# A transformer trunk on one core: the last two experts' rows by one-hot products, the other rows reloaded in two waves, the last norm on VectorE

## The chip, the core and the metric

The kernel runs on one core of a Trainium2 chip. Five engines work side by side: TensorE (products into eight PSUM banks of 128x512), VectorE, ScalarE, GpSimd (POOL) and SyncE (SP), which in this kernel only issues transfers. Each engine runs its own list of instructions in order and waits for the others through semaphores. The metric is the device time of one execution in microseconds, the median of several runs.

## The reference

One layer over 512 tokens of width 1024. After a mixer (pooling, chunked attention, a state space) comes a first LayerNorm, which gives h. The part that matters here is the second half:

```python
def moe(h, combine, w_gate, w_up, w_down):
    out = jnp.zeros_like(h)
    for e in range(N_EXPERTS):
        a = jax.nn.silu(h @ w_gate[e]) * (h @ w_up[e])
        out = out + combine[..., e:e + 1].astype(h.dtype) * (a @ w_down[e])
    return out
...
        combine = route(h, w_router, router_bias)
        ffn = moe(h, combine, w_exp_gate[i], w_exp_up[i], w_exp_down[i])
        ple = jax.nn.sigmoid(h @ w_ple_gate[i]) * (p[i] @ w_ple_proj[i])
        x = layer_norm(DN_ALPHA * h + ffn + ple, ln2_g[i], ln2_b[i])
```

There are 16 experts with an inner width of 256. route gives every token two experts and two weights that sum to one; combine is zero elsewhere. A token's ffn is therefore the weighted sum of two rows.

## The kernel before

The 512 tokens are four row tiles (t = 0 to 3) of 128 tokens. `xh` (region_f) holds alpha * h + ple of all four by the time the experts begin.

Each expert has room for 128 tokens (CAP); overflow goes to up to 7 extra rounds under `If(n_over > 0)`, which the inputs here do not enter. VectorE works out the slot of each (token, k) pair, k = 0 or 1 being the first and second expert of the token. GpSimd writes the pair's number 2 * token + k into `inv_d` at its slot with eight indirect transfers (line 530) and reads the list back as `inv_t`; `tok_t` is inv_t shifted right by one. For each expert GpSimd gathers the token rows of h from `h_d` (line 538) and, when the expert is done, scatters its 128 result rows to `ye_d` (expert_scratch) at the pair's number (line 543). Rows of ye_d are unweighted, and each is written by exactly one expert.

TensorE goes through the experts in a software pipeline: gate and up products of expert e (lines 1194 to 1207), the transposes of the tokens of e + 1 (1178), the down products of e - 1 (1222), the transposes of the activation of e (1212). fp32 operands are split into an upper and a lower part of a cheaper type (fp32r); ScalarE writes the upper parts (lines 797, 804, 819, 823), VectorE the lower ones (1664 to 1679). `step` is VectorE's share of one expert. The semaphore pe_dn counts finished down products. The results stand in banks 1 and 2 (B_DN), those of expert 15 in banks 4 and 5 (B_TOK). ScalarE copies them to `y_e` (line 831), expert e - 1 after its work for expert e. For expert 15 VectorE copies one half (1704) and ScalarE the other (844).

When the last scatter has landed, GpSimd sets moe_done, and SyncE reloads ye_d in eight transfers of 512 KB, one for each t and k (line 409). Then, per row tile: VectorE adds the two weighted rows to xh (`combine`, line 1728) and takes the mean; ScalarE squares and sums (`deviation`, 860) and takes the root (863). For tiles 0 and 1 ScalarE normalises (`x_hat`, 867) and VectorE multiplies by the gain and adds the bias (`affine`, 1746 and 1747); for tiles 2 and 3 VectorE does both with two instructions (1754, 1757) around a reciprocal. SyncE stores each tile (412). `ln_st`, `ln_mv`, `ln_rs` hold sum, mean and square sum, and root and its reciprocal.

## Time and profile before

| what | us |
|---|---|
| median of 3 runs | 471.43 (471.35 to 471.88) |
| the profiled execution | 470.61, its span 468.9 |
| TensorE busy | 426.5 (91%) |
| VectorE busy | 321.5 (69%) |
| ScalarE busy | 218.4 (47%) |
| GpSimd busy | 116.0 (25%) |
| share of the chain that ended last | TensorE 86%, VectorE 5%, ScalarE 3%, DMA 3% |

The span goes from the first to the last recorded instruction of the one profiled execution; the rest of its time lies around it. The chain is followed back from the last instruction, at each step to what released it. "Landing" is the time from a transfer's issue to its semaphore. Numbers in the sections below are of this one execution unless they are called a median.

### The profile page before, as it was taken

What the parts mean: (1) busy time and instruction counts of PE and PEld (TensorE: products, weight loads), DVE (VectorE), ACT (ScalarE), POOL (GpSimd) and SP (SyncE); (2) the same over time, 40 slices, a digit from 0 to 9 for tenths busy, and PEclk for the clock granted to TensorE, in tenths of its full rate; (3) what the DMA queues carried; (4) which work ended last, traced back from release to release, by engine and by line L of the source; (5) the groups of instructions that cost most, each with busy time, mean ns of one, the idle gap of its engine ahead of it and who ended that gap; (6) DMA issues with size and microseconds to landing.
All of it is one profiled execution on the core that took longest, in us unless ns stands there. A gap on an engine that the chain in (4) does not pass through costs nothing.

```text
span 468.9 us, 5180 instructions
## 1 busy us (share of the span) xinstructions
PE 426.5 (91%) x1837; PEld 280.1 (60%) x1837; DVE 321.5 (69%) x491; ACT 218.4 (47%) x361; POOL 116.0 (25%) x145
## 2 busy tenths in 40 slices
PE   6999999999999999999999999999999999999000
PEld 2444564496675544446687676777777777777000
DVE  3799959876343876667483257787767777777287
ACT  3111361053976800115110157788677787786151
POOL 7880051560085100000006500222332222212000
PEclk9999999999999999999999999999999999999655
DMA  8992032327965701112620249999999999610563
GB/s 275 381 365 91 0 52 71 75 89 217 414 266 198 295 0 45 45 46 67 254 83 0 54 166 426 407 422 419 408 374 364 390 370 389 249 72 16 184 258 144
DMA packets 36792, 98.95 MB, mean 211 GB/s; under 512 B 16049, under 2 KB 22081, under 8 KB 30113
## 3 DMA queue, kind: packets, MB, share of 16 engines
q1 hardware_dynamic: 27472, 88.01, 49.4%
q0 software_dynamic: 5600, 8.94, 5.7%
...
q14 instruction: 11, 0.08, 0.0%
...
## 4 chain that ended last, share of the span: by engine, by line
PE 86%; DVE 5%; ACT 3%; DMA 3%; issue 1%; SPq 0%; POOLq 0%; DVEq 0%
PE bank L885 12%; PE bank L1049 11%; PE bank L1222 10%; PE bank L1194 5%; PE bank L892 5%; PE bank L1199 4%; PE bank L1203 4%; PE bank L1207 4%; PE bank L1121 3%; PE bank L1123 3%; PE bank L1122 3%; PE bank L1135 3%; PE bank L1178 3%; PE bank L901 2%; DVE region_f L1728 2%; PE bank L910 2%
## 5 line engine op out<-in xcount | busy, mean ns | idle before, releaser
L1049 PE MATMUL bank<-region_b,region_e 128*128 128x512 f32 x128 | 58.3, 601 | 0.6 <-DVE region_f L1521 0.6
L885 PE MATMUL bank<-region_e,region_a 128*128 128x512 f32 x128 | 55.9, 595 | 0.0
L885 PEld LDWEIGHTS bank<-region_e,region_a 128*128 128x128 f32 x128 | 24.1, 190 | 29.4 <-issue 29.1
L1049 PEld LDWEIGHTS bank<-region_b,region_e 128*128 128x128 f32 x128 | 23.2, 191 | 25.0 <-issue 23.6
L1199 PE MATMUL bank<-gate_up_upper,tokens_upper 128*128 128x512 f32 x96 | 36.3, 459 | 0.0
L530 POOL DMA_INDIRECT slot_scratch<-io_t,slot_i x8 | 8.4, 1055 | 93.4 <-issue 93.4
L543 POOL DMA_INDIRECT expert_scratch<-region_g,inv_t x8 | 11.5, 1436 | 78.2 <-ACT region_g L831 78.2
L1672 DVE TENSOR_TENSOR gate_up_lower<-region_a,gate_up_upper 128x1024 fp32r<-128x1024 f32 x24 | 28.0, 1221 | 2.7 <-ACT gate_up_upper L804 2.7
L1203 PE MATMUL bank<-gate_up_upper,tokens_lower 128*128 128x512 f32 x96 | 29.8, 392 | 0.0
L892 PE MATMUL bank<-region_e,region_a 128*128 128x512 f32 x48 | 23.4, 651 | 4.7 <-DMA region_a<-in_w_in 4.7
L1121 PE MATMUL bank<-ple_gate_upper,hidden_upper 128*128 128x512 f32 x64 | 26.6, 415 | 0.0
L1521 DVE SCALAR_TENSOR_TENSOR region_f<-bank,rms_r,region_f 128x512 f32<-128x512 f32 x24 | 18.0, 750 | 11.6 <-PE bank L1049 11.0
L1123 PE MATMUL bank<-ple_gate_upper,hidden_lower 128*128 128x512 f32 x64 | 25.0, 391 | 0.0
L1122 PE MATMUL bank<-ple_gate_lower,hidden_upper 128*128 128x512 f32 x64 | 25.0, 390 | 0.0
L804 ACT ACTIVATE gate_up_upper<-region_a 128x1024 fp32r<-128x1024 f32 x24 | 23.7, 1058 | 2.6 <-DMA region_a<-in_w_exp_down 2.6
L1207 PE MATMUL bank<-gate_up_lower,tokens_upper 128*128 128x512 f32 x96 | 24.5, 391 | 0.0
L1199 PEld LDWEIGHTS bank<-gate_up_upper,tokens_upper 128*128 128x128 f32 x96 | 18.1, 189 | 10.4 <-issue 6.0
L543 POOL DMA_INDIRECT expert_scratch<-region_b,inv_t x8 | 10.2, 1276 | 49.4 <-ACT region_b L831 40.1
L772 ACT ACTIVATE ln_rs<-ln_mv,eps_t 128x1 f32<-128x1 f32 x4 | 1.2, 296 | 45.4 <-DVE ln_mv L1527 45.4
L768 ACT ACTIVATE region_h<-bank 128x512 f32<-128x512 f32 x8 | 4.8, 597 | 37.4 <-PE bank L1123 37.4
L901 PE MATMUL bank<-region_a,region_e 128*128 128x384 f32 x64 | 21.2, 488 | 0.0
L1203 PEld LDWEIGHTS bank<-gate_up_upper,tokens_lower 128*128 128x128 f32 x96 | 18.0, 188 | 4.0
...
## 6 DMA issues: line engine op xcount, KB each, us to landing
...
```

What stands on the lines that cost most here:

```text
L885: last = mm(bank[bank_i][:], w[:, k, m * P:(m + 1) * P], xT[:, k, :], start=(k == 0), stop=(k == KD - 1))
L892: last = mm(bank[m][:], w_ssm[:, k, m * P:(m + 1) * P], xT[:, k, :], start=(k == 0), stop=(k == KD - 1))
L901: last = mm(bank[bank_i][:, 0:ATT_W], xT[:, k, t * P:(t + 1) * P], w_v[:, k, :], start=(k == 0), stop=(k == KD - 1))
L1049: last = mm(bank[WO_AT[half][group]][:], hdT[:, k, t * P:(t + 1) * P], w_o[:, k, half * 512:half * 512 + 512], start=(i == 0), stop=(i == ...
L1121: mm(bank[PG_AT[k % 2]][:], h_hi[t][:, x], pg_hi[:, w], start=(c == 0), stop=False)
L1122: mm(bank[PG_AT[k % 2]][:], h_hi[t][:, x], pg_lo[:, w], start=False, stop=False)
L1123: last = mm(bank[PG_AT[k % 2]][:], h_lo[t][:, x], pg_hi[:, w], start=False, stop=(c == KD - 1))
L1199: mm(out_, x_hi[r][:, k * P:(k + 1) * P], w_hi[:, k], start=False, stop=False)
L1203: mm(out_, x_lo[:, k * P:(k + 1) * P], w_hi[:, k], start=False, stop=False)
L1207: last = mm(out_, x_hi[r][:, k * P:(k + 1) * P], w_lo[:, KD - KS + k], start=False, stop=(k == KS - 1))
L1222: last = mm(bank[banks[half]][:], x[r][:, k * P:(k + 1) * P], w[:, k * D + half * 512:k * D + half * 512 + 512], start=(i == 0), stop=(i = ...
L1672: tt(w_lo[:, :, at:at + 2 * DE], w[:, :, at:at + 2 * DE], w_hi[:, :, 2 * c * DE:2 * (c + 1) * DE], ALU.subtract).then_inc(S["gu_lo_set"], 1)
```

## The change

- The pair written to the slot list is now (number, weight), so that the list read back, `inv_w`, holds for each slot its weight. ScalarE's copies out of the banks (now lines 871 to 875) scale by it, and ye_d holds weighted rows.
- Experts 14 and 15 (LATE = 2) are not scattered. ScalarE writes the upper part of their weighted rows to `yl_hi`, VectorE the lower part to `yl_lo`. VectorE builds for each of the two a one-hot matrix `onehot` of 128 slots by 512 tokens from a row of token numbers, `t_iota`. TensorE multiplies them, for each row tile, into the banks of OH_BANKS.
- Since the rows of these two experts are no longer written, ye_d is filled with zeros first: a tile of zeros goes to `zero_d`, and eight transfers from there to ye_d stand in SyncE's list ahead of the stores of h.
- The reload begins when the scatters up to expert 13 have landed. First wave, on SyncE: both k of tiles 0 and 1, into `y_two` (k = 1) and `y_one` (k = 0). Second wave, when tile 0 is there: k = 1 of tiles 2 and 3 on SyncE, k = 0 of tiles 2 and 3 by two transfers of GpSimd that add to xh.
- y_two goes into the banks by products with the identity, ahead of the one-hot products of the same tile. y_one is added to xh by VectorE.
- combine adds a tile's two banks to xh with an accumulator. The norm of all four tiles is made with the two instructions that tiles 2 and 3 had; x_hat and affine are gone.

The diff, cut to its core:

```diff
 OVER = 7
+LATE = 2
...
+OH_BANKS = ((3, 6), (7, 0), (1, 2), (4, 5))
...
+        y_two = RB[:, 4096:8192].rearrange("p (t d) -> p t d", t=NT)
+        y_one = RA[:, 2048:4096].rearrange("p (t d) -> p t d", t=2)
+        t_iota = RH[:, 7168:7168 + T]
+        onehot = [over(f"onehot{i}", T, C0 + 4 * (8192 + i * T)) for i in range(LATE)]
+        yl_hi = [over(f"late_upper{i}", D, B0 + 4 * (2 * i * D)) for i in range(LATE)]
+        yl_lo = [over(f"late_lower{i}", D, B0 + 4 * ((2 * i + 1) * D)) for i in range(LATE)]
...
+            sp.dma_start(zero_d, RH[:, 3072:3072 + D]).then_inc(S["ye_zero"], 16)
+            sp.wait_ge(S["ye_zero"], 16)
             sp.wait_ge(S["kern_done"], 2)
...
+            for c in range(2 * NT):
+                sp.dma_start(ye_d[c * P:(c + 1) * P, :], zero_d).then_inc(S["ye_zero"], 16)
...
+            yv = ye_d.rearrange("(t p k) d -> t k p d", p=P, k=2)
+            sp.wait_ge(S["pe_dn"], NE - LATE)
+            for b in range(4):
+                sp.wait_ge(S[f"ye_out{b}"], 16 * ((NE - LATE - 1 - b) // 4 + 1))
+            for t in range(2):
+                sp.dma_start(y_two[:, t, :], yv[t, 1]).then_inc(S[f"y_in{t}"], 16)
+                sp.dma_start(y_one[:, t, :], yv[t, 0]).then_inc(S[f"y_in{t}"], 16)
+            sp.wait_ge(S["y_in0"], 32)
+            for t in range(2, NT):
+                sp.dma_start(y_two[:, t, :], yv[t, 1]).then_inc(S["y2_in"], 16)
...
-            sp.wait_ge(S["moe_done"], 1)
-            yv = ye_d.rearrange("(t p k) d -> t k p d", p=P, k=2)
-            for t in range(NT):
-                for k in range(2):
-                    sp.dma_start(RA[:, (2 * t + k) * D:(2 * t + k + 1) * D], yv[t, k]).then_inc(S[f"yk{k}_in{t}"], 16)
...
+            link(g.iota(t_iota, pattern=[[1, T]], base=0, channel_multiplier=0, allow_small_or_imprecise_dtypes=True))
...
-                if e == NE - 1:
-                    gp.wait_ge(S["ye_last"], 1)
-                    gp.wait_ge(S["ye_evac"], 2 * e + 1)
-                else:
+                if e < NE - LATE:
                     gp.wait_ge(S["ye_evac"], 2 * e + 2)
-                scatter(inv_t[:, e:e + 1], y_e[e % 4], f"ye_out{e % 4}")
+                    scatter(inv_i[:, e, 0:1], y_e[e % 4], f"ye_out{e % 4}")
             n_over = gp.value_load(over_i[0:1, 0:1], min_val=0, max_val=OVER)
             for b in range(4):
-                gp.wait_ge(S[f"ye_out{b}"], 16 * NE // 4)
+                gp.wait_ge(S[f"ye_out{b}"], 16 * ((NE - LATE - 1 - b) // 4 + 1))
+            gp.wait_ge(S["ple_done"], 2 * NT)
+            yv = ye_d.rearrange("(t p k) d -> t k p d", p=P, k=2)
+            gp.wait_ge(S["y_in0"], 32)
+            for t in range(2, NT):
+                gp.dma_start(xh[:, t, :], yv[t, 0], accum_op=ALU.add).then_inc(S[f"y_in{t}"], 16)
...
-                    a.activation(y_e[b][:, half * 512:half * 512 + 512], bank[B_DN[half]][:], ACT.Copy).then_inc(S["ye_evac"], 1)
+                    a.activation(y_e[b][:, half * 512:half * 512 + 512], bank[B_DN[half]][:], ACT.Copy,
+                                 scale=inv_w[:, e, 1:2]).then_inc(S["ye_evac"], 1)
+
+            def late_upper(i, half, banks):
+                a.activation(yl_hi[i][:, half * 512:half * 512 + 512], bank[banks[half]][:], ACT.Copy,
+                             scale=inv_w[:, NE - LATE + i, 1:2]).then_inc(S["yh_set"], 1)
...
-                if e >= 1:
+                if 1 <= e < NE - 1:
                     y_copy(e - 1, (0, 1))
-            ac.wait_ge(S["pe_dn"], NE + 1)
-            ac.wait_ge(S["ye_out3"], 16 * (NE // 4 - 1))
-            a.activation(y_e[3][:, 512:1024], bank[B_TOK[1]][:], ACT.Copy).then_inc(S["ye_evac"], 1)
+            ac.wait_ge(S["pe_dn"], NE - 1)
+            for half in range(2):
+                late_upper(0, half, B_DN)
+            for half in range(2):
+                ac.wait_ge(S["pe_dn"], NE + half)
+                late_upper(1, half, B_TOK)
...
-            def x_hat(t):
-                ac.wait_ge(S["rs2_ready"], t + 1)
-                a.activation(xh[:, t, :], xh[:, t, :], ACT.Identity, bias=ln_mv[:, t, 0:1], scale=ln_rs[:, t, 1:2]).then_inc(S["xhat_done"], 1)
-
             a.preload_act_table(ACT.Sqrt)
-            deviation(0)
-            deviation(1)
-            x_hat(0)
-            deviation(2)
-            x_hat(1)
-            deviation(3)
+            for t in range(NT):
+                deviation(t)
...
+            def to_tokens(t, half, i, start, stop):
+                for n_, y in enumerate((yl_hi[i], yl_lo[i])):
+                    last = mm(bank[OH_BANKS[t][half]][:], onehot[i][:, t * P:(t + 1) * P], y[:, half * 512:half * 512 + 512],
+                              start=(start and n_ == 0), stop=(stop and n_ == 1))
+                return last
+
+            def both_halves(t, i, stop):
+                for half in range(2):
+                    if i == 1 and t == 0:
+                        pe.wait_ge(S["yh_set"], 3 + half)
+                        pe.wait_ge(S["yl_set"], 5 + half)
+                    last = to_tokens(t, half, i, False, stop)
+                return last
+
+            for t in range(NT):
+                if t < 2:
+                    pe.wait_ge(S[f"y_in{t}"], 32)
+                else:
+                    pe.wait_ge(S["y2_in"], 32)
+                if t == NT - 1:
+                    pe.wait_ge(S["yh_set"], 4)
+                    pe.wait_ge(S["yl_set"], 6)
+                for half in range(2):
+                    mm(bank[OH_BANKS[t][half]][:], ident[:], y_two[:, t, half * 512:half * 512 + 512], start=True, stop=False)
+                if t == 0:
+                    pe.wait_ge(S["yh_set"], 2)
+                    pe.wait_ge(S["yl_set"], 4)
+                both_halves(t, 0, False)
+                both_halves(t, 1, True).then_inc(S["pe_dn"], 1)
...
+                link(tt(pair_w[:, :, k, 1], wgt[:, k, :], wsum, ALU.mult))
+            link(v.tensor_copy(pair_i[:, :, 0], io_t[:]))
...
+            def late_lower(i, half, banks):
+                dv.wait_ge(S["yh_set"], 2 * i + half + 1)
+                cols = slice(half * 512, half * 512 + 512)
+                stt(yl_lo[i][:, cols], bank[banks[half]][:], inv_w[:, NE - LATE + i, 1:2], yl_hi[i][:, cols],
+                    ALU.mult, ALU.subtract).then_inc(S["yl_set"], 1)
+
             for e in range(NE - 4, NE):
                 step(e, e % 4, last=(e == NE - 1))
-            dv.wait_ge(S["pe_dn"], NE)
-            dv.wait_ge(S["ye_out3"], 16 * (NE // 4 - 1))
-            v.tensor_copy(y_e[3][:, 0:512], bank[B_TOK[0]][:]).then_inc(S["ye_last"], 1)
+                if e < NE - 2:
+                    i = e - (NE - 4)
+                    ts(onehot[i][:], t_iota, tok_f[:, i:i + 1], None, ALU.is_equal).then_inc(S["yl_set"], 1)
+            for i, banks in enumerate((B_DN, B_TOK)):
+                for half in range(2):
+                    late_lower(i, half, banks)
+            for t in range(2):
+                dv.wait_ge(S[f"y_in{t}"], 32)
+                if t == 0:
+                    dv.wait_ge(S["ple_done"], 2 * NT)
+                tt(xh[:, t, :], xh[:, t, :], y_one[:, t, :], ALU.add).then_inc(S["one_added"], 1)
+            dv.wait_ge(S["one_added"], 2)
...
             def combine(t):
 
-                for k in range(2):
-                    dv.wait_ge(S[f"yk{k}_in{t}"], 16)
-                    yk = RA[:, (2 * t + k) * D:(2 * t + k + 1) * D]
-                    link(stt(xh[:, t, :], yk, wgt[:, k, t:t + 1], xh[:, t, :], ALU.mult, ALU.add,
-                             accum_out=ln_st[:, t, 0:1] if k == 1 else None))
-                ts(ln_mv[:, t, 0:1], ln_st[:, t, 0:1], -1.0 / D, None, ALU.mult).then_inc(S["z2_ready"], 1)
-
-            def scale_rows(t):
-
+                if t >= 2:
+                    dv.wait_ge(S[f"y_in{t}"], 16)
+                dv.wait_ge(S["pe_dn"], NE + 1 + t + 1)
+                for half in range(2):
+                    cols = slice(half * 512, half * 512 + 512)
+                    link(stt(xh[:, t, cols], bank[OH_BANKS[t][half]][:], 1.0, xh[:, t, cols], ALU.mult, ALU.add,
+                             accum_out=ln_st[:, t, half:half + 1]))
+                ts(ln_mv[:, t, 0:1], ln_st[:, t, 0:1], ln_st[:, t, 1:2], -1.0 / D, ALU.add, ALU.mult).then_inc(S["z2_ready"], 1)
+
+            def centred(t):
+                return RE[:, t * D:(t + 1) * D]
+
+            def centre(t):
+                dv.wait_ge(S["z2_ready"], t + 1)
+                link(stt(centred(t), xh[:, t, :], ln_mv[:, t, 0:1], lng2, ALU.add, ALU.mult))
+
+            def scale(t):
                 dv.wait_ge(S["ln_sqrt"], NT + t + 1)
                 link(v.reciprocal(ln_rs[:, t, 1:2], ln_rs[:, t, 0:1]))
-                tt(ln_mv[:, t, 0:1], ln_mv[:, t, 0:1], ln_rs[:, t, 1:2], ALU.mult).then_inc(S["rs2_ready"], 1)
+                stt(xh[:, t, :], centred(t), ln_rs[:, t, 1:2], lnb2, ALU.mult, ALU.add).then_inc(S["o_dve"], 1)
 
             combine(0)
+            centre(0)
+            scale(0)
             combine(1)
-            scale_rows(0)
+            centre(1)
+            scale(1)
             combine(2)
-            scale_rows(1)
-
-            def affine(t):
-                dv.wait_ge(S["xhat_done"], t + 1)
-                link(tt(xh[:, t, :], xh[:, t, :], lng2, ALU.mult))
-                tt(xh[:, t, :], xh[:, t, :], lnb2, ALU.add).then_inc(S["o_dve"], 1)
-
-            affine(0)
+            centre(2)
             combine(3)
-            affine(1)
-            for t in range(2, NT):
-                xg = RE[:, (t - 2) * D:(t - 1) * D]
-                link(stt(xg, xh[:, t, :], ln_mv[:, t, 0:1], lng2, ALU.add, ALU.mult))
-                dv.wait_ge(S["ln_sqrt"], NT + t + 1)
-                link(v.reciprocal(ln_rs[:, t, 1:2], ln_rs[:, t, 0:1]))
-                stt(xh[:, t, :], xg, ln_rs[:, t, 1:2], lnb2, ALU.mult, ALU.add).then_inc(S["o_dve"], 1)
+            scale(2)
+            centre(3)
+            scale(3)
```

SyncE's end of list. Before, behind the overflow block, which itself waits for all down products:

```order
L395 REGISTER_ALU
L395 COMPARE_AND_BRANCH
L394 UNCONDITIONAL_BRANCH
L409 DMA region_a<-expert_scratch 128x1024 [waits moe_done]
L409 DMA region_a<-expert_scratch 128x1024 x7
L412 DMA out<-region_f 128x1024 [waits o_dve] x4
```

Now, from the last weight load on, ahead of that block:

```order
L408 DMA region_c<-in_w_exp_down 128x2048 [waits pe_dn]
L415 DMA region_b<-expert_scratch 128x1024 [waits ye_out2,ye_out1,ye_out3,ye_out0,pe_dn]
L416 DMA region_a<-expert_scratch 128x1024
L415 DMA region_b<-expert_scratch 128x1024
L416 DMA region_a<-expert_scratch 128x1024
L419 DMA region_b<-expert_scratch 128x1024 [waits y_in0]
L419 DMA region_b<-expert_scratch 128x1024
```

The reloads moved ahead of the overflow block and of the wait for the last down product; they wait for the scatters (ye_out0 to ye_out3, one per buffer) instead.

VectorE before, from the first reloaded tile on:

```order
L1728 SCALAR_TENSOR_TENSOR region_f<-region_a,wgt,region_f 128x1024 [waits yk0_in0,ln2_in]
L1728 SCALAR_TENSOR_TENSOR region_f,ln_st<-region_a,wgt,region_f 128x1024 [waits yk1_in0,dve_step]
L1730 TENSOR_SCALAR ln_mv<-ln_st 128x1 [waits dve_step]
L1728 SCALAR_TENSOR_TENSOR region_f<-region_a,wgt,region_f 128x1024 [waits yk0_in1]
L1728 SCALAR_TENSOR_TENSOR region_f,ln_st<-region_a,wgt,region_f 128x1024 [waits yk1_in1,dve_step]
L1730 TENSOR_SCALAR ln_mv<-ln_st 128x1 [waits dve_step]
L1735 RECIPROCAL ln_rs<-ln_rs 128x1 [waits ln_sqrt]
L1736 TENSOR_TENSOR ln_mv<-ln_mv,ln_rs 128x1 [waits dve_step]
L1728 SCALAR_TENSOR_TENSOR region_f<-region_a,wgt,region_f 128x1024 [waits yk0_in2]
L1728 SCALAR_TENSOR_TENSOR region_f,ln_st<-region_a,wgt,region_f 128x1024 [waits yk1_in2,dve_step]
```

VectorE now, after its last lower part of the expert phase (region_a is y_one), and from the first combine on (late_upper_83 and late_lower_85 are expert 14's parts, the next numbers expert 15's):

```order
L1777 SCALAR_TENSOR_TENSOR late_lower_85<-bank,region_h,late_upper_83 128x512 [waits yh_set] x2
L1777 SCALAR_TENSOR_TENSOR late_lower_86<-bank,region_h,late_upper_84 128x512 [waits yh_set] x2
L1792 TENSOR_TENSOR region_f<-region_f,region_a 128x1024 [waits ple_done,y_in0]
L1792 TENSOR_TENSOR region_f<-region_f,region_a 128x1024 [waits y_in1]
L1794 TENSOR_LOAD over_i [waits one_added]
```

```order
L1821 SCALAR_TENSOR_TENSOR region_f,ln_st<-bank,region_f 128x512 [waits pe_dn,ln2_in]
L1821 SCALAR_TENSOR_TENSOR region_f,ln_st<-bank,region_f 128x512 [waits dve_step]
L1823 TENSOR_SCALAR ln_mv<-ln_st 128x1 [waits dve_step]
L1830 SCALAR_TENSOR_TENSOR region_e<-region_f,ln_mv,region_h 128x1024 [waits z2_ready]
L1834 RECIPROCAL ln_rs<-ln_rs 128x1 [waits ln_sqrt,dve_step]
L1835 SCALAR_TENSOR_TENSOR region_f<-region_e,ln_rs,region_h 128x1024 [waits dve_step]
L1821 SCALAR_TENSOR_TENSOR region_f,ln_st<-bank,region_f 128x512 [waits pe_dn]
```

Two reads of reloaded rows per tile became one read of two banks, and the load of the overflow count (TENSOR_LOAD over_i) now stands behind the two sums that wait for the reload.

TensorE before ended with the down products of expert 15:

```order
L1222 MATMUL bank<-down_upper_last,act_upper_78 128x512 x2
L1222 MATMUL bank<-down_lower_72,act_upper_78 128x512 x2
L1222 MATMUL bank<-down_upper_last,act_lower_80 128x512 x2
L1275 TENSOR_LOAD over_i
L1275 ISA x2
L1278 COMPARE_AND_BRANCH [waits ye_last,ye_evac]
```

Now its list goes on behind the overflow block (region_b is y_two; tile 0 and the start of tile 1):

```order
L1316 UNCONDITIONAL_BRANCH
L1355 MATMUL bank<-region_b,ident 128x512 [waits y_in0]
L1355 MATMUL bank<-region_b,ident 128x512
L1334 MATMUL bank<-late_upper_83,onehot_81 128x512 [waits yl_set,yh_set]
L1334 MATMUL bank<-late_lower_85,onehot_81 128x512
L1334 MATMUL bank<-late_upper_83,onehot_81 128x512
L1334 MATMUL bank<-late_lower_85,onehot_81 128x512
L1334 MATMUL bank<-late_upper_84,onehot_82 128x512 [waits yl_set,yh_set]
L1334 MATMUL bank<-late_lower_86,onehot_82 128x512
L1334 MATMUL bank<-late_upper_84,onehot_82 128x512 [waits yl_set,yh_set]
L1334 MATMUL bank<-late_lower_86,onehot_82 128x512
L1355 MATMUL bank<-region_b,ident 128x512 [waits y_in1]
```

Four such groups of ten stand there, one per row tile.

## Rows read from the trace of the kernel before

**Rows 1.** Windows: busy us of each engine, granted clock, DMA share, GB/s.

```profile
434.08:439.08 5.00, 0.00 (x1) 0.00 (x0) 0.00 (x0) 1.88 (x2) 0.97 (x1) 0.73 0.29 115
...
442.43:465.82 23.39, 0.00 (x0) 0.00 (x0) 21.21 (x30) 8.41 (x14) 0.00 (x0) 0.50 0.55 212
465.82:468.90 3.08, 0.00 (x0) 0.00 (x0) 0.00 (x1) 0.00 (x0) 0.00 (x0) 0.50 0.42 170
```

**Rows 2.** Chain of waits: start us, us, what; from the last scatter on.

```profile
435.55 3.19 DMA expert_scratch<-region_b,inv_t
...
439.08 0.33 SPq L409
...
439.93 6.85 DMA region_a<-expert_scratch
...
446.81 1.28 DVE region_f L1728
...
448.17 1.30 DVE region_f L1728 x2
```

**Rows 3.** Timeline: start us, us, engine, line; the last experts.

```profile
418.36 0.41 DVE L1658 TENSOR_TENSOR region_c<-region_c,bank 128x256 f32<-128x256 f32 x1
...
426.50 1.43 POOL L543 DMA_INDIRECT expert_scratch<-region_g,inv_t  x1 [7.19 <-ACT region_g L831]
...
434.12 0.60 ACT L844 ACTIVATE region_b<-bank 128x512 f32<-128x512 f32 x1 [2.12 <-PE bank L1222]
435.54 1.28 ACT L869 ACT_TABLE_LOAD   x1 [0.83 <-issue]
```

**Rows 4.** Tile expert_scratch, 426 to 427: landing of expert 13's scatter alone.

```profile
DMA to landing us min/median/max: 3.6/3.6/3.6
```

**Rows 5.** Timeline: one tile's sums and norm, and a last product.

```profile
442.43 2.61 DVE L1728 SCALAR_TENSOR_TENSOR region_f<-region_a,wgt,region_f 128x1024 f32<-128x1024 f32 x2 [8.98 <-DMA region_a<-expert_scratch]
...
445.08 0.15 DVE L1730 TENSOR_SCALAR ln_mv<-ln_st 128x1 f32<-128x1 f32 x1
...
446.54 0.30 ACT L863 ACTIVATE ln_rs<-ln_mv,eps_t 128x1 f32<-128x1 f32 x1
...
461.82 1.28 DVE L1757 SCALAR_TENSOR_TENSOR region_f<-region_e,ln_rs,region_h 128x1024 f32<-128x1024 f32 x1
```

**Rows 6.** VectorE's groups by form: count, busy us, mean ns, idle before.

```profile
L1521 DVE SCALAR_TENSOR_TENSOR region_f<-bank,rms_r,region_f 128x512 f32<-128x512 f32 x24 | 18.0, 750 | 11.6 <-PE bank L1049 11.0
...
L1747 DVE TENSOR_TENSOR region_f<-region_f,region_h 128x1024 f32<-128x1024 f32 x2 | 2.4, 1224 | 0.1
```

**Rows 7.** Chain of waits: products of both kinds on TensorE.

```profile
266.18 0.23 PE bank L1122
...
266.64 3.43 PE bank L1135 x8
```

**Rows 8.** Line 409: landing of the eight reloads.

```profile
DMA to landing us min/median/max: 3.3/8.1/10.6
```

**Rows 9.** Windows of TensorE: its busy us, granted clock, DMA share, GB/s.

```profile
436.40:436.60 0.20, 0.00 (x0) 0.54 0.00 0
```

**Rows 10.** Waits of SyncE: us in total, times, longest.

```profile
SPq L310 <- ACT region_c L658: 39.8, 1, 39.8
```

**Rows 11.** Windows, all engines: the stretch after expert 0's first loads.

```profile
165.00:170.00 5.00, 4.40 (x14) 1.97 (x13) 3.51 (x6) 0.57 (x3) 0.00 (x0) 1.00 0.00 0
```

**Rows 12.** Timeline: SyncE's stores of h, VectorE, the first gather, its reader.

```profile
176.88 42.95 SPq L369 DMA_DIRECT2D h_scratch<-region_f  x4
...
221.45 0.69 DVE L1543 SCALAR_TENSOR_TENSOR region_f<-region_f,region_h 128x512 f32<-128x512 f32 x1
...
263.89 1.45 POOL L538 DMA_INDIRECT region_e<-h_scratch,tok_t  x1 [4.56 <-DVE tok_t L1649]
...
269.91 1.05 PE L1178 MATMUL bank<-ident,region_e 128*128 128x128 f32 x8
```

**Rows 13.** Tile region_e, GpSimd, 263 to 265: landing of the first gather.

```profile
DMA to landing us min/median/max: 4.6/4.6/4.6
```

58 lines of the change are left out of this document (40 added, 18 removed).

## Prediction

> **What bounds the kernel now.** I read the page's list of engines first. TensorE is busy for nine tenths of the span, so the body of the kernel is TensorE's and only the end can be anyone else's. The windows of the last 40 us show where that stops: TensorE ends at 434.08, five us follow in which VectorE does nothing, VectorE is then busy for 21.2 of 23.4 us, and the last 3.1 us are a store alone [rows 1]. The chain of waits names the steps: the last expert's rows are sent to memory (435.55, 3.19 us to landing), SyncE then issues the reloads from 439.08, the third of them takes 6.85 us, and from 446.81 the chain is VectorE to 465.82 [rows 2]. Before 434 the chain is the experts' matmuls without a gap worth naming. So a gain can come from three things only: when the reload starts, how long VectorE works after it, and the last store.
>
> **The change: the reload.** Before, the reload waits for the last scatter. Now it waits for expert 13's. That scatter is issued at 426.50 and lands 3.6 us later [rows 3, 4], so the first wave is issued at 430.15 instead of 439.08. Its four transfers of 512 KB have the first four of the eight as their measure: the third landed 7.73 us after the first issue (446.81 - 439.08), the fourth no later than 448.11, where its reader begins (448.17 less the two short steps between), or 9.03 us [rows 2]. Token tile 1 is complete at 430.15 + 7.73 to 9.03 = 437.9 to 439.2; I take 438.4, nearer the low end, because only four transfers share the engines instead of eight. Tile 0 is complete by about 430.15 + 4.6 = 434.8 (VectorE's two reads of it in before began 442.43 and about 443.7) [rows 5]. Nothing else uses the DMA engines then: the weight loads are over.
>
> The late evacuations: ScalarE's last one ends at 434.72, as before [rows 3]. VectorE's lower part of it is a 128x512 product from a bank, 0.75 us by the same kind of instruction [rows 6], so it ends at 435.5. It replaces a copy of about the same length. Then VectorE adds tile 0 (1.22 us, a 128x1024 sum [rows 6]), to 436.8, and waits for tile 1: 438.4 + 1.25 = 439.65. Then it loads the overflow count and branches. No row of VectorE shows that price; ScalarE's same pair stands as 0.83 us of idle before its table load [rows 3]. The bounds are 0 and 0.83; I take 0.83, since nothing here reads ahead of the wait. The first product sum therefore starts at 440.5 and not at 442.43.
>
> **VectorE's work.** A row tile now costs two 128x512 sums from banks with accumulator (0.75 and 0.08 to read it, and gaps of 0.04), and a 0.15 us scalar: 1.95 us. Before it was 2.80 (442.43 to 445.23) [rows 5]. Centring is one 1.28 us instruction; ScalarE's square, its accumulator and its root are over at 446.84, and the sum ended at 445.23: 1.61 us and a gap of 0.03, 1.64 [rows 5]. So for tiles 0 and 1, where VectorE waits for the root before it goes on, a tile is 1.95 + 1.64 + 1.50 (reciprocal, as short as the scalar's 0.15, last product 1.28, and gaps [rows 5]) = 5.09, twice 10.2. For tiles 2 and 3 the order is sum 2, centre 2, sum 3, scale 2, centre 3, scale 3, and the root of tile 3 is hidden by 2.8 us of work: 1.95 + 1.34 + 1.95 + 1.50 + 1.31 + 1.47 = 9.5. Together 19.7 us against the 23.4 of before. The end is 440.5 + 19.7 = 460.2, and the store adds 3.08 as before [rows 1]: **a span of 463.3 against 468.9, 5.6 us less**.
>
> **What must hide for that.** TensorE now makes 8 fp32 identity products and 32 one-hot products. By the chain a fp32 product of this size takes 3.43 / 8 = 0.43 us and one of the split kind 0.23 [rows 7]. A tile is 2 x 0.43 + 8 x 0.23 = 2.7 us. Tile 0's products wait for the last lower part (435.5) and end near 437.5, three us before VectorE wants them at 440.5. Tile 1 starts at 438.4 and ends 441.1, wanted at 445.6. The second wave (tiles 2 and 3) is issued at 434.8 by SyncE and GpSimd. Before, the last of the eight reloads was issued at 442.5 and landed at most 10.6 us later [rows 8], so all 4 MB were there 14.0 us after the first issue; the same from 430.15 is 444.2. VectorE wants tile 2 at 440.5 + 10.2 = 450.7 and tile 3 at 454.0. So the two adding transfers have 7 us of room. No row shows such a transfer. From below its price is that of a plain GpSimd transfer alone, 3.2 to 3.6 us [rows 2, 4]; from above I allow three times that after a start at 436, 447, still in time.
>
> The clock is the second cover. TensorE's granted clock fell from 1.0 to 0.5, from the level of 2.4 GHz to that of 1.2, at about 436.5, when the engine had done nothing for 2.4 us [rows 9]. Here it pauses 0.7 us at 434.1 and about 1 us at 437.5, so I expect the high level through tile 1. If it falls, a tile takes some 5.4 us (twice the rows above, an estimate): tile 1 ends 443.8, tile 2 449.2, tile 3 454.6, which VectorE wants at 454.0. That costs 0.6 us, not more.
>
> The Trainium skill, "TensorE: Matmul & The Clock Gate" (the part on HAM oscillation), says that work in bursts shorter than the wait between them runs at the low level every time. By that rule all four tiles would be slow and the end 0.6 us later, 463.9 instead of 463.3; the trace shows one such fall, after one long pause, and bears the rule out only so far.
>
> **Edits earlier in the kernel, taken at nothing.** The fill of the scratch tensor: one 512 KB store of zeros early on SyncE, ahead of copies for which SyncE had waited 39.8 us anyway [rows 10], and eight 512 KB copies from memory to memory before the stores of h. DMA was idle from 165 to 170 [rows 11]; the stores of h were issued from 176.88, and VectorE's first use of what they guard is at 221.45 [rows 12]. 4 MB read and written from 165 at the latest may last 50 us before anyone waits. The pair of slot and weight: one more VectorE copy (some 0.2 us) and a wider payload of 8 bytes in the same number of pieces. The first gather was issued at 263.89 and landed 4.6 us later, 268.5; TensorE reaches its tokens at 269.91 [rows 12, 13]. 1.4 us of cover, of which 0.2 is used. The weight as ScalarE's scale costs nothing that I can see. The two one-hot builds (at most the 0.75 us of the 128x512 form in [rows 6]) stand on VectorE after steps 12 and 13. VectorE had no pause before 418.36 [rows 3], so the next product is up to 0.75 us later; TensorE wants it only after the twelve down products that stand ahead, 12 x 0.23 = 2.8 us [rows 7].
>
> **The rivals.**
> First, **the products for tiles 2 and 3 become the bound**: low clock and a late second wave together. For it: TensorE's work comes in four bursts, and the second wave is shared by two queues. If the plain half of it lands at 446 and not by 444.2, tile 2 ends 451.4 and tile 3 456.8, against 454.0: +2.8. With clock alone +0.6. Time 466.4 to 468.6.
> Second, **the other side: adding transfers that crawl**. The place is VectorE's sum of tile 3, behind GpSimd's second transfer. The gain is gone when that one lands at 454.0 + 5.6 = 459.6, 23 us after its issue, against 3.2 for a plain one: seven times slower. At 27 us the kernel takes 475. Nothing in the profile speaks for seven times, but nothing shows the operation either.
> Third, **the head pays**: copies from memory to memory so slow that the h stores land after 221, or the slot list comes back over 1.4 us later. Each further us is one us on TensorE. With 1 to 3 us of this: 466.8 to 468.8; a loss needs 5.6.
> Fourth, **the early reload does not happen early**, since one of SyncE's waits before it is later than I read: then only VectorE's 23.4 - 19.7 = 3.7 us are gained, 467.7.
>
> **How the numbers follow.** The profiled execution took 470.61 with its span of 468.9; the median of the three runs is 471.43, and I take 5.6 us from that: 471.43 - 5.6 = **465.8**. Chances: forecast 0.64 (464.3 to 467.0), first rival 0.16, second 0.08 (of which 0.05 ends slower than before), third 0.07 (0.02 slower), fourth 0.05. The low end: no price for the count (-0.8) and tile 1 at 437.9 (-0.5), together 464.5, and 0.2 for the spread of the runs. The high end takes in the first and fourth rival: 468.6. A measurement of this kernel can tell about 0.2% from no change, 0.94 us, so same means 470.5 to 472.4. Faster 0.88, same 0.05, slower 0.07.
>
> **What would show it.** The first reload issued within half a us of 430.2; VectorE's first sum from a bank at 440 to 441 and its last instruction near 460.2; pauses of VectorE between the sums of tiles 2 and 3 under 1 us, ended by ScalarE and not by TensorE or a DMA; a granted clock of 1.0 to about 441; TensorE's last down product still at 434.1. Wrong would be a last down product later than 434.5 (then the head or the one-hot builds cost), a wait of VectorE for region_f from the scratch tensor (adding transfers), or one for a bank (TensorE).

## The result, and the profile after

The changed kernel takes 464.56 us (median of 4 runs, 463.55 to 464.59), the kernel before 471.39 beside it (4 runs, 471.04 to 471.88). The ratio of the runs is 0.9849 with a 95% interval of 0.9833 to 0.9864: 7.1 us faster (6.4 to 7.9; the medians alone differ by 6.8), where 5.6 was forecast. The profiled execution took 464.56 with a span of 462.8, against 470.61 and 468.9: 6.1 us of span.

First the windows of the changed kernel's last 28 us (columns as in [rows 1]): from the last down product to VectorE's first sum from a bank, from there to VectorE's end, and the last store.

```profile
434.90:441.38 6.48, 5.17 (x18) 3.13 (x17) 3.27 (x5) 1.97 (x2) 1.89 (x2) 1.00 0.92 304
441.38:459.76 18.38, 9.65 (x33) 5.76 (x31) 17.02 (x32) 6.14 (x12) 0.00 (x0) 0.95 0.55 159
459.76:462.80 3.04, 0.00 (x0) 0.00 (x0) 0.00 (x0) 0.00 (x0) 0.00 (x0) 0.50 0.43 172
```

Set beside [rows 1], the 23.39 us from VectorE's first sum to its end have become 18.38, and its busy time 17.02 instead of 21.21. The gap ahead is shorter too (6.48 against 8.35, from 434.08 to 442.43), though this execution's last down product ended 0.8 us later than before's. The last store is as it was. Counted from the last down product, 5.0 us are gained in the stretch and 1.9 in the gap ahead of it.

The chain of waits of the changed kernel, from the issue of the fourth reload on (start, us, what; to be read beside [rows 2]):

```profile
432.25 6.59 DMA region_a<-expert_scratch
438.87 1.24 DVE region_f L1792
...
440.13 0.56 DVEq L1794
...
440.73 0.22 DVEq L1794
...
441.38 0.71 DVE region_f L1821 x2
442.11 0.71 DVE region_f L1821 x2
442.84 0.23 DVE ln_mv L1823
443.09 1.25 ACT region_a L908 x2
...
458.48 1.28 DVE region_f L1835
```

The first bank sum is only 1.05 us earlier than the first sum of before, though the reload starts 8.15 us earlier. Before, VectorE began 3.35 us after the first issue, with tile 0, and waited for tile 1 in between; now it waits for tile 1 (7.9 us after the first issue), adds it (1.24) and loads the count (1.28), 10.45 us in all. What is bought with the longer way to the first sum is a shorter stretch after it.

By the timeline the first reload was issued at 430.93 ([rows 2] had 439.08). In the chain, the second half of tile 1's rows lands at 438.84, and between the add and the first bank sum stand 1.28 us in which VectorE's queue (DVEq) loads the overflow count. The timeline shows the same places on the two engines (start, us, engine, line; in brackets the idle time before, and what ended it):

```profile
436.22 1.98 PE L1355 MATMUL bank<-region_b,ident 128*128 128x512 f32 x4 [1.31 <-DMA region_a<-expert_scratch]
...
438.87 1.23 DVE L1792 TENSOR_TENSOR region_f<-region_f,region_a 128x1024 f32<-128x1024 f32 x1 [1.32 <-DMA region_a<-expert_scratch]
...
441.38 0.69 DVE L1821 SCALAR_TENSOR_TENSOR region_f<-bank,region_f 128x512 f32<-128x512 f32 x1 [1.28 <-issue]
...
441.99 0.08 DVE L1821 DVE_READ_ACCUMULATOR region_f<-bank,region_f 128x1 f32 x1
...
442.11 0.69 DVE L1821 SCALAR_TENSOR_TENSOR region_f<-bank,region_f 128x512 f32<-128x512 f32 x1
...
442.84 0.21 DVE L1823 TENSOR_SCALAR ln_mv<-ln_st 128x1 f32<-128x1 f32 x1
...
445.45 1.98 PE L1355 MATMUL bank<-region_b,ident 128*128 128x512 f32 x4 [1.82 <-DMA region_b<-expert_scratch]
```

Two readings matter below. A bank sum begins 0.73 us after the other (442.11 - 441.38), and its 0.08 us accumulator read lies inside the 0.69. And TensorE stood idle for 1.82 us before tile 2, since the second wave landed at 445.4 (issued 436.6 at the latest, 8.8 us to landing; 444.2 had been allowed). In this execution nobody paid for that.

### The profile page after: what moved, and what is told of

It reads as the page before. It is cut to its first block, busy times and chain, and to the rows that moved or that the text cites. A ratio compares the mean times of both kernels' runs of the same rounds, so it can differ in the third digit from the quotient of the medians.

```text
span 462.8 us, 5294 instructions
## 1 busy us (share of the span) xinstructions
PE 441.7 (95%) x1885; PEld 288.9 (62%) x1885; DVE 323.0 (70%) x502; ACT 219.8 (47%) x360; POOL 114.0 (25%) x146
## 3 DMA queue, kind: packets, MB, share of 16 engines
q10 hardware_dynamic: 3696, 1.71, 1.4%
## 4 chain that ended last, share of the span: by engine, by line
PE 87%; DVE 5%; ACT 4%; DMA 2%; issue 1%; SPq 0%; DVEq 0%
PE bank L925 12%; PE bank L1089 12%; PE bank L1262 9%; PE bank L1234 6%; PE bank L932 5%; PE bank L1239 4%; PE bank L1243 4%; PE bank L1247 4%; PE bank L1161 3%; PE bank L1163 3%; PE bank L1162 3%; PE bank L1175 3%; PE bank L1218 3%; PE bank L941 2%; PE bank L950 2%; PE bank L1004 1%
## 5 line engine op out<-in xcount | busy, mean ns | idle before, releaser
L925 PEld LDWEIGHTS bank<-region_e,region_a 128*128 128x128 f32 x128 | 24.1, 190 | 29.4 <-issue 29.2
L557 POOL DMA_INDIRECT slot_scratch<-region_h,slot_i x8 | 8.4, 1055 | 92.8 <-issue 92.8
L570 POOL DMA_INDIRECT expert_scratch<-region_g,region_h x8 | 10.0, 1253 | 80.1 <-ACT region_g L871 80.1
L1239 PEld LDWEIGHTS bank<-gate_up_upper,tokens_upper 128*128 128x128 f32 x96 | 18.1, 189 | 10.4 <-issue 6.2
L932 PEld LDWEIGHTS bank<-region_e,region_a 128*128 128x128 f32 x48 | 10.1, 213 | 17.7 <-issue 12.8
## 6 DMA issues: line engine op xcount, KB each, us to landing
region_a<-in_w_exp_down SPq DMA_DIRECT2D x8, 1024.0 KB, 17.7
region_a<-in_w_in SPq DMA_DIRECT2D x3, 1536.0 KB, 17.2
```

The lines of the kernel that those rows point to most:

```text
L925: last = mm(bank[bank_i][:], w[:, k, m * P:(m + 1) * P], xT[:, k, :], start=(k == 0), stop=(k == KD - 1))
L932: last = mm(bank[m][:], w_ssm[:, k, m * P:(m + 1) * P], xT[:, k, :], start=(k == 0), stop=(k == KD - 1))
L1239: mm(out_, x_hi[r][:, k * P:(k + 1) * P], w_hi[:, k], start=False, stop=False)
```

## Experiments

Spans and waits are those of each kernel's one profiled execution, medians are of all its runs. The kernel before stood beside each group of runs with medians of 470.59 to 471.22. The first profile of the changed kernel is the one above, the second that of the run below.

### The changed kernel again

> The changed kernel itself, again, beside the three parts that follow. Theory A (the gain is 6.9 us: 4.0 from the sums and the start of the reload, the rest from VectorE's shorter list, and the 0.8 us by which the profile of before began and ran ahead belongs to the execution, not to the kernel): 6.5 to 7.2 us below before. Theory B (the changed kernel pays 0.8 us in its first 400 us, by the fill or the slot pairs): 6.0 us below before, and its trace again has the first reload issued at 430.9.

464.85 us (4 runs, 464.57 to 465.80; ratio 0.986, 0.9841 to 0.9878). The profiled execution is the slowest of the four, with a span of 464.0, and it shows what the first did not. Its timeline, and windows of 1 us of TensorE alone (busy us, granted clock, DMA share, GB/s):

```profile
446.00 2.90 PE L1355 MATMUL bank<-region_b,ident 128*128 128x512 f32 x4 [2.88 <-DMA region_b<-expert_scratch]
...
451.58 0.69 DVE L1821 SCALAR_TENSOR_TENSOR region_f<-bank,region_f 128x512 f32<-128x512 f32 x1 [1.17 <-PE bank L1334]
```

```profile
444.00:445.00 1.00, 0.00 (x0) 1.00 1.08 213
445.00:446.00 1.00, 0.00 (x1) 1.00 1.08 217
446.00:447.00 1.00, 1.00 (x3) 0.96 1.03 221
447.00:448.00 1.00, 1.00 (x4) 0.50 0.98 356
```

The second wave landed 0.6 us later (446.0), TensorE had been idle for 2.88 us, the granted clock fell from 1.00 to 0.50 (2.4 to 1.2 GHz) as it began, and VectorE waited 1.17 us for tile 2 and 0.59 for tile 3. That is the first rival, at work in one execution and not in the other. VectorE's two waits are 1.76 us, and its stretch is 20.19 us instead of 18.38. They come from the clock and not directly from the late landing: at the high level a tile takes 3.7 us, so that tile 2 would have been ready at 449.7, and VectorE asked for it at 450.41.

Of the two theories, the first reload at 430.30 and not 430.9 again speaks for A: the 0.8 us belong to the execution. The gain itself, 6.4 us by the medians and 6.6 by the ratio, does not decide it.

### The two halves of the end: the norm, and the reload

The norm alone, in the kernel before (the same edit of VectorE's and ScalarE's norm as in the change):

```
             combine(0)
+            centre(0)
+            scale(0)
             combine(1)
-            scale_rows(0)
+            centre(1)
+            scale(1)
             combine(2)
-            scale_rows(1)
+            centre(2)
...
```

> The kernel before with one part alone: the norm of tiles 0 and 1 made by VectorE's two instructions, sums and reload as before. Theory A: per tile 2.80 for the sums, 1.71 to the root, 1.49 for the rest, in the order of the changed kernel, from 442.43: the last instruction ends at 465.6 and not 465.8, so no change (0.2 us less). Rival: handing tiles 0 and 1 to ScalarE was itself the loss, and this alone gives 2 us or more.

470.58 us (11 runs), ratio 0.998, 0.9967 to 0.9994: 0.9 us. VectorE's stretch from first sum to end is 22.88 us instead of 23.39, but its busy time in it 21.50 instead of 21.21. The new norm is no lighter. Nor is the 0.9 us shown to be its gain: in the same group a kernel that only does more work (the fill, below) reads 1.2 us below the kernel before.

The old norm, in the changed kernel (VectorE's part of the edit; ScalarE normalises tiles 0 and 1 again):

```
             combine(0)
-            centre(0)
-            scale(0)
             combine(1)
-            centre(1)
-            scale(1)
+            scale_rows(0)
             combine(2)
-            centre(2)
+            scale_rows(1)
...
+            affine(0)
             combine(3)
...
```

> The changed kernel with the old norm for tiles 0 and 1 (ScalarE normalises, VectorE multiplies and adds, in the old order, in which the sums of tile 2 stand ahead of the gain of tile 0). Theory A: VectorE then wants tile 2's products at 445.6, TensorE has them at 449.1, and four long instructions stand where two did: the end 3.9 us later than the changed kernel, 468.4 in time. Rival (parts add up, and the norm alone is worth 0.2): 464.8.

466.98 us (5 runs, 466.22 to 469.30), 2.1 above the changed kernel in the same group, so neither the 3.9 of my theory nor the 0.2 of the rival. The profiled execution (469.30, span 467.5) is the slowest of them, by one line of its timeline:

```profile
450.75 0.69 DVE L1829 SCALAR_TENSOR_TENSOR region_f<-bank,region_f 128x512 f32<-128x512 f32 x1 [6.17 <-PE bank L1342]
```

The old order asks for tile 2 at 444.6, and TensorE, idle for 2.57 us until the second wave landed at 445.17 and then at a granted clock of 0.52, had it at 450.7. At the high level it would have had it at 448.9, so some 4.3 us of the wait are the landing's and 1.9 the clock's (an estimate from a tile's 3.7 us). VectorE's busy time between its first sum and its end is 16.83 us, with the new norm 17.02. So the old norm's price lies in waits for TensorE.

The reload at the old time (SyncE waits for the last expert before the first wave):

```
-            sp.wait_ge(S["pe_dn"], NE - LATE)
+            sp.wait_ge(S["pe_dn"], NE + 1)
```

> The changed kernel with the first wave of the reload held back until the last down product is done, all else the same. Theory A: the first reload is issued at about 435.2 and not 430.93, all that follows on VectorE moves with it: 4.0 to 4.3 us slower than the changed kernel, 468.7. Rival (VectorE's list is what counts, the reload has slack): under 2 us slower.

468.77 us (6 runs), ratio 0.9954, 0.9938 to 0.9970, 3.9 above the changed kernel's 464.85 (the groups' kernels before differ by 0.6; by the ratios it is 4.4). The first reload left at 435.29. TensorE idles 5.33 us and works through tile 0 at the low level, and VectorE waits for it:

```profile
440.58 3.78 PE L1355 MATMUL bank<-region_b,ident 128*128 128x512 f32 x4 [5.33 <-DMA region_a<-expert_scratch]
...
446.49 0.69 DVE L1821 SCALAR_TENSOR_TENSOR region_f<-bank,region_f 128x512 f32<-128x512 f32 x1 [1.76 <-PE bank L1334]
```

Of the 7.1 us, then, 4 to 5 hang on the early reload. With the late one the kernel is still 2.2 us below the kernel before (1.4 to 2.9), and its stretch from the first bank sum to VectorE's end is 18.39 us as in the changed kernel. That these 2 to 3 us are VectorE's smaller sums and their order is read from the stretch; no run has the smaller sums alone.

### The head: the fill alone

The kernel before with the store of zeros and the eight copies added to it:

```
+            sp.dma_start(zero_d, RH[:, 3072:3072 + D]).then_inc(S["ln2_in"], 16)
...
+            for c in range(2 * NT):
+                sp.dma_start(ye_d[c * P:(c + 1) * P, :], zero_d).then_inc(S["ln2_in"], 16)
```

> The kernel before with one part alone: the store of a tile of zeros and the eight copies of it to the scratch tensor, which the scatters then overwrite. Theory A: no change, within 0.2 us of before. Theory B: 0.6 to 0.8 us slower, since the first loads or the copies of the kernels into region_h wait behind the store.

470.16 us (8 runs), ratio 0.9974, 0.9962 to 0.9986. The fill costs nothing that this run shows (why it reads 1.2 us below the kernel before is open). The changed kernel's copies landed 9.9 to 17.7 us after issues at 155.9 to 160.3, so by 178; the stores of h behind them begin at 177.48 (before: 176.88), and VectorE's first use of what those guard is at 221.45 in [rows 12].

The other edit of the head, the pair of slot and weight, had no run of its own, but the traces price it. From GpSimd's first write to the slot list to TensorE's first product on gathered tokens it is 24.18 us in the kernel before (245.73 to 269.91) and 24.18 in the changed one (246.33 to 270.51).

The last down product ended at 434.90 in the first execution of the changed kernel, and 434.38 in the second, against 434.08 in [rows 1]. Over the eleven profiles with the changed body it ended between 433.55 and 435.25, over the three with the body of before at 434.08, 434.64 and 434.84. The 0.8 us lies within the spread between executions. Most of it is there early: TensorE's first products run from 4.68 to 28.05 before and from 4.88 to 28.64 in the changed kernel. No cost of the change shows in it.

### The overflow count

VectorE loads the count ahead of its two adds instead of behind them, in the changed kernel.

```
+            n_over = dv.value_load(over_i[0:1, 0:1], min_val=0, max_val=OVER)
             for t in range(2):
                 dv.wait_ge(S[f"y_in{t}"], 32)
...
             dv.wait_ge(S["one_added"], 2)
-            n_over = dv.value_load(over_i[0:1, 0:1], min_val=0, max_val=OVER)
```

> The changed kernel with VectorE's load of the overflow count moved ahead of its two waits for the reload. Theory A: the 1.28 us between the second sum and the first sum from a bank (440.10 to 441.38) are that load and its branch; ahead of the wait they are hidden, and the end comes 1.2 us sooner, 463.3. Rival: TensorE's products of tile 0 end at 440.06 and the wait for them, not the load, fills that time: no change.

463.42 us (5 runs, 462.53 to 463.66; 463.3 was expected), ratio 0.9841, 0.9825 to 0.9857. What ended the wait before the first bank sum is now the add itself:

```profile
439.34 0.69 DVE L1821 SCALAR_TENSOR_TENSOR region_f<-bank,region_f 128x512 f32<-128x512 f32 x1 [0.34 <-DVE region_f L1793]
```

0.34 us in place of 1.28: 0.94 of the 1.28 went with the load's new place, and it stood on the path, since the stretch after it is 18.38 us as before. TensorE's tile 0 was done in time, which refutes the rival. By medians the gain is 1.4 us against another group's changed kernel, by ratios 0.9; the ratios' intervals overlap.

### The form of the bank sum

The same sum with its factor 1.0 read from a column of ones, not given in the instruction:

```
-            link(stt(xh[:, t, cols], bank[OH_BANKS[t][half]][:], 1.0, xh[:, t, cols], ALU.mult, ALU.add,
+            link(stt(xh[:, t, cols], bank[OH_BANKS[t][half]][:], ones[:, 0:1], xh[:, t, cols], ALU.mult, ALU.add,
```

> The changed kernel with the factor 1.0 of the eight sums from banks read from a column of ones instead of standing in the instruction. Theory A: the instruction then takes 0.75 us like the form I priced it by, and not 0.69: 8 x 0.06 = 0.5 us more. Rival (0.75 was for another reason, such as the output or neighbours on the memory): no change, 0.69 stays.

465.04 us (4 runs), ratio 0.9878, 0.9860 to 0.9896; the intervals of this and of the changed kernel overlap, so the 0.5 us is read from the timeline:

```profile
440.76 0.75 DVE L1821 SCALAR_TENSOR_TENSOR region_f<-bank,ones,region_f 128x512 f32<-128x512 f32 x1 [1.36 <-issue]
...
441.44 0.08 DVE L1821 DVE_READ_ACCUMULATOR region_f<-bank,ones,region_f 128x1 f32 x1
...
441.56 0.75 DVE L1821 SCALAR_TENSOR_TENSOR region_f<-bank,ones,region_f 128x512 f32<-128x512 f32 x1
...
442.35 0.21 DVE L1823 TENSOR_SCALAR ln_mv<-ln_st 128x1 f32<-128x1 f32 x1
```

0.75 us, the duration of [rows 6], whose instruction has a column for its factor as well. From the start of the first sum to that of the scalar it is 1.59 us here and 1.46 in the changed kernel: 0.13 a tile, 0.5 us for four. The stretch is 19.17 us instead of 18.38; besides the 0.5, VectorE waited 0.34 us for tile 3, since TensorE, after a pause of 1.90 us, ran most of tile 2 at the low level.

### The adding transfers

GpSimd's two transfers write to another buffer without adding; the rows k = 0 are missing from tiles 2 and 3. The new line is shown simplified.

```
-                gp.dma_start(xh[:, t, :], yv[t, 0], accum_op=ALU.add).then_inc(S[f"y_in{t}"], 16)
+                gp.dma_start(RA[:, (2 + t) * D:(3 + t) * D], yv[t, 0]).then_inc(S[f"y_in{t}"], 16)
```

> The changed kernel with GpSimd's two adding transfers made plain ones, into another region; the rows they bring are left out of the sum of tiles 2 and 3. It prices the adding. Theory A: adding halves what the DMA engines move (205 to 221 GB/s at a full share from 443 to 447), so these two land in 7 to 8 us instead of 10.1 and 12.0, SyncE's half of the wave lands before 443.5 instead of 445.4, and the time stays, since VectorE waits for neither. Rival: the adding transfers delay the stores or VectorE's accesses, and the end comes 0.5 us or more sooner.

464.18 us (4 runs), ratio 0.9857 beside the changed kernel's 0.986, so the time stayed, as the theory had it. Landings of GpSimd's two transfers, from the first profile of the changed kernel, from the second, and without the addition:

```profile
DMA to landing us min/median/max: 10.1/11.0/12.0
```

```profile
DMA to landing us min/median/max: 11.5/12.7/14.0
```

```profile
DMA to landing us min/median/max: 8.3/8.6/9.0
```

The windows show what the DMA engines moved meanwhile (first the changed kernel, then without the addition; GB/s is the last column): with DMA engines at a full share both times, little more than half as much is moved while transfers add.

```profile
443.00:445.00 2.00, 0.63 (x3) 0.19 (x1) 1.54 (x4) 1.54 (x3) 0.00 (x0) 1.00 1.06 217
```

```profile
441.00:443.00 2.00, 2.00 (x10) 1.42 (x8) 1.90 (x6) 0.28 (x1) 0.00 (x0) 1.00 0.99 381
```

SyncE's second wave suffers with them: it landed 7.4 us after its last issue here, 8.8 and 9.9 in the two profiles of the changed kernel, 8.0 to 9.6 in the other kernels that add in this way. So the adding transfers don't crawl (the second rival needed 23 us), VectorE never waited for one, and what they cost they cost TensorE, whose tile 2 they delay.

### The second wave at once

SyncE issues tiles 2 and 3 behind the first four reloads, without waiting for tile 0.

```
-            sp.wait_ge(S["y_in0"], 32)
             for t in range(2, NT):
                 sp.dma_start(y_two[:, t, :], yv[t, 1]).then_inc(S["y2_in"], 16)
```

> The changed kernel, but SyncE issues the two reloads for tiles 2 and 3 right behind the first four instead of waiting until tile 0 has landed (about 432.7 in place of 435.7 to 436.2). GpSimd's adding transfers still wait for tile 0. Theory (in one execution of the changed kernel VectorE waited 1.17 us for TensorE's tile 2, in the other not at all, because the second wave, landed at 445.4 to 446.0, left TensorE idle for 1.8 or 2.9 us, and only after the longer gap the granted clock was 0.50): the second wave now lands by about 442, TensorE goes from tile 1 to tile 2 with under 0.5 us idle, the clock stays at 1.00 until tile 3 is done, VectorE waits for neither tile, and the span is 461.8 to 462.8, the lower of the changed kernel's spans. Rival A (the six loads share the queues): tiles 0 and 1 land 1.3 to 2.6 us later, and the span is 464 to 465.5. Rival B (the gap is not what the clock follows): the clock falls in 445 to 449 here too and VectorE waits for tile 2 as before, span 464.

463.89 us (5 runs, 463.55 to 464.13), ratio 0.9848, 0.9834 to 0.9862; span 462.4. The timeline, and the windows over it:

```profile
443.14 1.98 PE L1354 MATMUL bank<-region_b,ident 128*128 128x512 f32 x4
```

```profile
445.00:449.00 4.00, 4.00 (x16) 2.60 (x14) 3.61 (x7) 1.53 (x3) 0.00 (x0) 1.00 0.62 188
```

TensorE goes from tile 1 to tile 2 without a pause, the clock stays at 1.00 until tile 3 is done, and VectorE waits for no bank. Tile 1's add began at 438.43, so the six loads don't hinder the first four by more than 0.3 us (8.3 us after the first issue; 7.9 in the changed kernel). Both rivals fell. One part of the theory missed: the second wave was expected by 442 and landed at 443.1, 10.4 us after an issue at 432.7, just as TensorE came free. The lowest time stays where it was, and no run was above 464.13. That the dearer executions are gone is not shown by five runs: the kernel before, which has no second wave, spread over 1.9 us in this group and 2.8 in another.

Next, the count early and another order on VectorE (each tile's sums ahead of the scaling of the one before), the second wave still waiting:

```
             centre(0)
-            scale(0)
             combine(1)
+            scale(0)
             centre(1)
-            scale(1)
             combine(2)
+            scale(1)
```

> The changed kernel with VectorE's load of the overflow count ahead of its adds, and VectorE's norm in the order sums 0, centre 0, sums 1, scale 0, centre 1, sums 2, scale 1, and so on, so that each root is taken beside a tile's sums. The second wave still waits for tile 0. Theory 1 (VectorE's own busy time sets the end): three waits for roots of 0.39 us go, 1.2 us less than the 460.8 of the kernel with the count alone moved, span 459.6 to 460.1. Theory 2 (the second wave sets it now): the sums of tile 2 are wanted at about 446.7 where TensorE, as in the kernel with the old norm, is idle for over 2 us before tile 2, its clock falls to 0.5, tile 2 is done only at 448 to 450.7, and VectorE waits 1.5 to 4 us: span 461 to 463.5, no better than the kernel with the count alone moved or worse. I lean to theory 1 if tile 2's reload lands by 444, as in that kernel, and to theory 2 if by 445 or later.

463.38 us (5 runs, 462.20 to 465.70), ratio 0.9828, 0.9811 to 0.9844: no better than the count alone. The profiled execution is the slowest (span 463.9, expected by the second theory 461 to 463.5), and shows what that theory describes:

```profile
445.19 2.83 PE L1355 MATMUL bank<-region_b,ident 128*128 128x512 f32 x4 [2.36 <-DMA region_b<-expert_scratch]
...
450.80 0.69 DVE L1821 SCALAR_TENSOR_TENSOR region_f<-bank,region_f 128x512 f32<-128x512 f32 x1 [3.59 <-PE bank L1334]
```

The wait is as long as the 3.5 us between its fastest and its slowest run; whether the faster runs lacked it is not shown, since only the slowest was profiled. VectorE asked at 447.21. At the high level tile 2 would have been ready at 448.9, so about half of the wait is the landing's and half the clock's. I leaned on the landing (444 or 445) to decide between the theories, and it landed at 445.2.

The same kernel with the second wave at once:

> The kernel with the count loaded early and the interleaved norm, and besides the second wave issued at once, without the wait for tile 0. Expected if the second wave was what VectorE waited for and the six loads don't delay tiles 0 and 1: TensorE works through tiles 0 to 3 with under 0.5 us idle at a granted clock of 1.00, VectorE waits for at most 0.5 us of it, from its first bank sum at about 439.3 to its end 17.2 us, store 3.04: span 459.3 to 459.9, some 11 us under the kernel before. Rival (six loads share the queues and tile 1 lands 1.3 us later or more): the first bank sum begins at 440.6 or later and the span is 461 to 462.

462.62 us (5 runs, 462.06 to 463.39), ratio 0.9827, 0.9811 to 0.9843, the fastest median of the study. From first bank sum to VectorE's end 17.43 us (17.2 was expected), TensorE not waiting before tile 2 (its products begin at 443.26 behind tile 1). The span, 460.7, is 0.8 above the expected range, because the first sum began at 440.27 and not at 439.3. It began when tile 1 had landed and was added: the first reload was issued at 430.41, 0.83 us later than in the kernel with the count alone, and tile 1 landed 8.3 us after it, 0.1 later than there. In this stretch the new order is worth 1.0 us (18.39 with the wave at once and the old order of sums).

Last, whether the new norm is worth its price once the second wave is early: the old norm with the wave at once.

> The changed kernel with the norm of before (its steps shared with ScalarE, in the order of before), and the second wave issued at once. With the old norm and the wave as in the change the span was 467.5, and VectorE waited 6.17 us for TensorE's tile 2 (wanted at 444.6, ready at 450.7), since the second wave landed at 445.1 and the granted clock then stood at 0.52. Theory (most of what the new norm was worth, 3.5 us against the 464.0 of the changed kernel, is that it does not ask for tile 2 so early, and not that it takes less of VectorE's time): with the wave issued at once TensorE has tile 2 ready at about 446.9 at a clock of 1.00, VectorE waits 2 to 2.5 us instead of 6.17, and the span is 463.4 to 464.2, so that the new norm is worth only 1.0 to 1.8 us against the 462.4 of the changed kernel with the wave issued at once. Rival (the old norm costs its 3.5 us in work of VectorE): 465.6 to 466.2.

465.72 us (4 runs, 465.29 to 466.06), ratio 0.9889, 0.9869 to 0.9909; span 464.1, in the expected 463.4 to 464.2. VectorE's wait for tile 2 is down from 6.17 to 2.25:

```profile
447.26 0.69 DVE L1828 SCALAR_TENSOR_TENSOR region_f<-bank,region_f 128x512 f32<-128x512 f32 x1 [2.25 <-PE bank L1341]
```

By profiled spans the new norm is worth 1.7 us with the early wave and 3.5 with the late one (467.5 - 464.0). The medians don't bear out the second figure: 466.98 - 464.85 = 2.1 late, 465.72 - 463.89 = 1.8 early. So the theory holds for the executions that were profiled, and for the kernel on the whole the new norm is worth about 2 us either way. In both, its worth is the order: VectorE's busy time is 16.82 us with the old norm and 17.02 with the new, and what the old norm adds is waits.

## The prediction, step by step

**The reload.** Expert 13's scatter landed, and the first reload left at 430.93, forecast 430.15; 430.30 in the second profile. Tile 1 landed 7.9 us after the first issue (forecast 8.25, bounds 7.73 to 9.03), tile 0 5.2 us after (forecast 4.6). These terms hold. The fourth rival is refuted: the reload is early, and putting it back costs 4 to 5 us.

**The overflow count.** It was taken at what was called its upper bound, 0.83, and measured 1.28. The bound was ScalarE's, and no bound for VectorE's queue; moving the load took 0.94 us away. 0.45 us too little in the sum.

**VectorE's work: the step that failed.** "Two 128x512 sums from banks with accumulator (0.75 and 0.08 to read it, and gaps of 0.04), and a 0.15 us scalar: 1.95 us." It measured 1.67 (441.38 to 443.05, where the scalar ends). The mechanism was right, and this term of the sum was too large. Two mistakes went the same way. The 0.08 stands inside the product's 0.69, as [rows 5] could have told (442.43 and 2.61 us, and the scalar already at 445.08, with no room for another 0.08); and the 0.75 of [rows 6] is the price of a factor from a column, 0.06 more than this instruction's constant, as the run with the column shows. The scalar, with a column and a constant, is 0.21 and not 0.15, which gives 0.06 back. Four times 0.28 is 1.1 us, most of the difference between 19.7 and the 18.38 that VectorE took. The other terms of a tile hold: the root at 1.71 against 1.64, last product and reciprocal 1.49 against 1.50.

**The sum again**, with the measured terms: 463.3 forecast, + 0.8 for this execution's later experts, - 0.35 for tile 1's landing, + 0.45 for the count, - 1.3 for VectorE, is 462.9, and the span was 462.8. The last store held (3.04 for 3.08). Against the median, the later experts are no part of it: they are in the medians of both kernels. From the medians: 5.6 forecast, + 0.35 - 0.45 + 1.3, is 6.8 us, which is what they differ by. The forecast of 465.8 was 1.2 us above the median and its range began at 464.3, which is where 471.43 times the ratio lies: too little was left below, since the low end held only the count, the landing and 0.2 for the spread, and no doubt about VectorE's own term. That the sum came out only 0.5 us above the measured span is partly luck: the later experts and the count hid two thirds of what VectorE's term had too much.

**What was to hide.** TensorE's tile took 3.7 us (436.22 to 439.89), not 2.7. A tile has two identity products and the timeline records four, so a record is half of such a product: the 3.43 / 8 of [rows 7] was the price of a half, and a tile is 4 x 0.43 + 8 x 0.24 = 3.6 us. Tile 0's products ended at 440.06 and not at 437.5. In the first profile it cost nothing, since VectorE loaded the count until 441.3 and wanted tile 1 at 446.17, whose products ended at 443.6. The clock stayed at 1.00 through tile 1, as forecast, and in the first profile to the end; the one-hot builds took 0.48 us each at 409.18 and 419.19 with no product late.

**The first rival** (0.16, priced at 466.4 to 468.6) is real and was overpriced at up to 2.8 us: it is 1.8 us of VectorE's stretch in one of two profiles of the changed kernel. The forecast itself had the cause slightly wrong. It allowed the second wave until 444.2 and the adding transfers until 447, as separate items; they share the DMA engines, and both come late (445.4 and 449.4). Here TensorE's pauses before tile 0 (1.07 to 1.67 us) never brought the low level, and one of 5.33 us with the late reload did. Those before tile 2 were followed by it at 1.90, 2.36, 2.57 and 2.88 us and not at 0.29, 0.42, 0.98 and 1.82. The length of a pause does not decide it alone: after TensorE's last product the level stayed at 1.00 for 4 us and more in the first profile and with the early count, and for 2.3 us in the kernel before ([rows 9] is the fall). The Trainium skill's "TensorE: Matmul & The Clock Gate" (the part on HAM oscillation) tells of bursts of work shorter than the wait for data between them, each of which starts cold. The prediction applied that to its own pauses of 0.7 and 1 us between tiles of 2.7 us, which are not such a case; every pause here but the 5.33 us was shorter than a tile's 3.7 us, so the runs hardly test it.

**The other rivals.** Adding transfers landed in 10.1 to 14.0 us in the two profiles, about three to four times the 3.2 to 3.6 of a plain one alone (the forecast allowed three times), with no wait of VectorE. But the comparison with one alone misleads: plain ones in the same company took 8.3 to 9.0. The head paid nothing. The other side, slower than before, appeared in no run.
